# Two of four token tiles project their input from one read of the weights, the second tile's results going through DRAM

## What is computed

```python
proj = rms_norm(h, ln1_g) @ w_in            # [512, 1024] @ [1024, 4096]
u_s5, q, k, v, gate_logits = split(proj)    # 512, 1024, 256, 256, 2048
gates = sigmoid(gate_logits + b_gate)
y_s5 = s5_mixer(u_s5, ...) @ w_s5_branch    # a scan over the tokens
y_attn = sliding_window_attention(q, k, v, ...) @ w_attn_branch
h = h + (g_s5 * y_s5 + g_attn * y_attn) @ w_out
xn2 = rms_norm(h, ln2_g)
# peer_mixer: 8 heads x 16 experts per token, picked by top-k over sub keys
a = einsum('cd,ced->ce', xn2, u_tab[expert])
h = h + einsum('ce,ced->cd', gate * gelu(a), v_tab[expert])
```

## Time and profile before

| what | value |
|---|---|
| runs shown | 3314.36, 3316.03, 3311.30 us; median 3314.36 |
| the profiled execution | 3312.03 us, its span 3310.2 us |
| PE busy, DVE busy | 2458.2 us (74%), 2320.8 us (70%) |
| ACT busy, POOL busy | 1331.3 us (40%), 1137.1 us (34%) |
| DMA | 1295.01 MB, mean 391 GB/s |
| of this, gathers of expert rows | 1076.50 MB, 80.5% of 16 engines' span |
| of this, SP's queue | 213.81 MB, 17.0% |
| chain that ended last | PE 36%, DMA 24%, DVE 22%, issue 10% |

### The profile page before, as it was taken

One profiled execution on the slowest core, in us unless ns is written; L12 is line 12 of the kernel. 1 busy time (PEld: TensorE's weight loads), 2 busy tenths in 40 slices (PEclk: granted clock), 3 DMA queues, 4 the chain that ended last, 5 costly groups with the idle time before them and its releaser, 6 DMA issues.

```text
span 3310.2 us, 40579 instructions
## 1 busy us (share of the span) xinstructions
PE 2458.2 (74%) x14052; PEld 1048.5 (32%) x14052; DVE 2320.8 (70%) x5500; ACT 1331.3 (40%) x3603; POOL 1137.1 (34%) x1038
## 2 busy tenths in 40 slices
PE   7969779786797777879687859778886655555554
PEld 3533333223332233336343426423333211111111
DVE  7429783878738787475975685888866777777644
ACT  2114442444424443243473343368733443333322
POOL 0002342323323243232343343444433444444432
PEclk9979779897898978989888879878888877777877
DMA  8899999999999999999999999999999999999997
GB/s 245 305 354 381 411 384 404 414 409 404 380 403 417 412 396 395 410 375 407 376 370 384 387 395 385 406 416 418 383 405 364 412 420 419 418 413 411 420 420 323
DMA packets 214057, 1295.01 MB, mean 391 GB/s; under 512 B 26934, under 2 KB 30294, under 8 KB 82776
## 3 DMA queue, kind: packets, MB, share of 16 engines
q0 software_dynamic: 148320, 1076.50, 80.5%
q1 hardware_dynamic: 64860, 213.81, 17.0%
q10 hardware_dynamic: 672, 2.12, 0.2%
HBM read 1289.62 MB, written 2.71 MB: 390 GB/s over the span
## 4 chain that ended last, share of the span: by engine, by line
PE 36%; DMA 24%; DVE 22%; issue 10%; ACT 5%; POOL 3%; POOLq 0%; another core or an unknown queue 0%; ACTq 0%; DVEq 0%
PE ps L1714 11%; PE ps L1794 10%; DMA ring<-in_k_uv,idx 10%; DVE ring L413 9%; DMA ring<-in_k_vu,idx 8%; DMA wsl<-in_k_wu 5%; PE ps L2088 5%; POOL ring L2392 3%; PE ps L2098 2%; DVE big L466 2%; ACT L1242 2%; PE ps L1771 1%; PE ps L1969 1%; ACT diag L1242 1%; DMA wsl<-in_k_wmod 1%
## 5 line engine op out<-in xcount | busy, mean ns | idle before, releaser
L1714 PE MATMUL ps<-ring,diag 64*64 64x512 f32 x8192 | 1259.0, 742 | 490.6 <-ACT diag L1242 468.8
L413 DVE CUSTOM_DVE_ANT_0 ring<-ring,xn 128x1024 f32<-128x1024 f32 x1024 | 1237.4, 1220 | 483.7 <-DMA ring<-in_k_vu,idx 259.7
L2392 POOL DMA_INDIRECT ring<-in_k_vu,idx x514 | 566.9, 1103 | 1145.4 <-DVE aw L413 637.1
L2392 POOL DMA_INDIRECT ring<-in_k_uv,idx x510 | 564.1, 1106 | 969.2 <-DVE aw L413 671.7
L1714 PEld LDWEIGHTS ps<-ring,diag 64*64 64x64 f32 x8192 | 313.9, 158 | 1264.3 <-ACT diag L1242 736.6
L1242 ACT ACTIVATE aw<-aw 128x2 f32<-128x2 f32 x512 | 103.6, 202 | 1085.8 <-DVE aw L413 1081.8
L1794 PE MATMUL ps<-wsl,xT 128*128 128x512 f32 x896 | 428.2, 621 | 34.0 <-DMA wsl<-in_k_wu 29.2
L1242 ACT ACT_TABLE_LOAD x340 | 436.2, 1283 | 21.2 <-issue 9.3
L1242 ACT ACTIVATE diag<-gid,aw 128x64 f32<-128x64 f32 x1024 | 311.3, 342 | 298.9 <-PE ps L1714 281.7
L1242 ACT ACTIVATE gid<-ident,gate 128x64 f32<-128x64 f32 x1024 | 292.5, 332 | 0.0
L1794 PEld LDWEIGHTS ps<-wsl,xT 128*128 128x128 f32 x896 | 165.9, 196 | 294.8 <-issue 230.1
(11 more groups left out here) (264 smaller groups left out, 2127.8 us busy)
## 6 DMA issues: line engine op xcount, KB each, us to landing
wsl<-in_k_wu SPq DMA_DIRECT2D x342, 512.0 KB
wsl<-in_k_wmod SPq DMA_DIRECT2D x40, 512.0 KB
ring<-in_k_vu,idx POOLq DMA_INDIRECT x514
ring<-in_k_uv,idx POOLq DMA_INDIRECT x510
ring<-in_k_wmod SPq DMA_DIRECT2D x8, 512.0 KB, 10.0
wsl<-in_k_wu SPq DMA_DIRECT2D x8, 280.0 KB
hres<-in_x SPq DMA_DIRECT2D x4, 512.0 KB, 6.0
pers<-L1d POOLq DMA_DIRECT2D x8, 256.0 KB, 15.7
```

The lines of the kernel that those rows point to most:

```text
L413: V(v.tensor_tensor_reduce(u_row(s), u_row(s), xn[:, n % 3, :], 1.0, 0.0, ALU.mult, ALU.add, aw[:, b, k:k + 1]), ("dot", s))
L1714: r = t.matmul(PA[half][64 * q:64 * q + 64, :], diag[64 * half:64 * half + 64, s % (2 * PAIR), :], v_row(s)[64 * half:64 * half + 64, 512 ...
L2392: Q(p.indirect_dma_start(out=both_rows(s), out_offset=None, in_=tab, in_offset=bass.IndirectOffsetOnAxis(ap=idx[:, n % 2, k:k + 1], axis=0 ...
```

## The change

Tile 3's input projection is done with tile 2's. Its norm follows tile 2's (into a second buffer `xT3`), and the new `project_two` multiplies each unit first with tile 2's, then with tile 3's tokens, banks 4, 5 and 2, 3. ScalarE evicts tile 3's block into one of two buffers (`going`: half of `xr`, and `uT`), waits for its own write and issues a DMA of 256 KB to DRAM (`keptd`). The 32 win units of tile 3 leave the list. SP brings the eight blocks back once tile 2's query has been transposed (so that `xr` is free), ahead of tile 3's first weight, in nine DMAs (block 3 is two). VectorE's copy into `uT` waits for the last two blocks written.

Tiles 2 and 3 get tables of their own: tile 2 from slot 116 to 253, tile 3 from 253 to 360.

```diff
-L1_PARTS = (("norm", 4), ("win", 25), ("qk", 7), ("mid", 48), ("branch", 13), ("route", 10), ("top", 15))
+SHARED_PARTS = (("norm", 5), ("win", 42), ("qk", 7), ("mid", 47), ("branch", 13), ("route", 10), ("top", 13))
+KEPT_PARTS = (("win", 22), ("qk", 6), ("mid", 44), ("branch", 11), ("route", 9), ("top", 15))
...
-        units = [(n,) + u for n in (0, 1, 2, 3, 4, 6) for u in weight_units(n // 4)]
+        units = [(n,) + u for n in (0, 1, 2, 3, 4, 6) for u in weight_units(n // 4) if (n, u[0]) != (3, "win")]
...
-            parts = FIRST_PARTS if n == 1 else L1_PARTS
-            x = (0, -1, 116, 238)[n]
+            parts = (FIRST_PARTS, FIRST_PARTS, SHARED_PARTS, KEPT_PARTS)[n]
+            x = (0, -1, 116, 253)[n]
...
             def u_turned(n):
                 V.stage("qk")
                 V.wait_ge("uT_t", n)
+                if n == 2:
+                    V.wait_ge("kept", 6)
+                    V.wait_ge("kept", 7)
                 V(v.tensor_copy(uT, P3(0)), ("uT", n))
...
+                    if n == 3:
+                        continue
                     S.stage("win")
...
+                    if n == 2:
+                        if b >= 2:
+                            S.wait_ge("kept", b - 2)
+                        S(act(going[b % 2], PS[2 + b % 2], ACT.Copy if b < 4 else ACT.Sigmoid), ("going", b))
+                        S.wait_own()
+                        Q(a.dma_start(keptd[b], going[b % 2]), "kept%d" % (b % 2), ("kept", b))
...
+            def project_two():
+                mine = [u for u in units if u[0:2] == (2, "win")]
+                for k, (_, _, b, u, nk, _, _, nn, _) in enumerate(mine):
+                    pace(2, "win", (k // 2 * 2) / len(mine))
...
+                    for lhsT, bank in ((xT, 4 + b % 2), (xT3, 2 + b % 2)):
+                        if b >= 4 and u == 0:
+                            t.matmul(PS[bank], ones[0:1, :], gt[0:1, 512 * (b - 4):512 * (b - 3)], start=True, stop=False)
+                        for j in range(2):
+                            r = t.matmul(PS[bank], lhsT[:, 2 * u + j, :], wsl[:, at % NWS, j, :],
+                                         start=(u + j == 0 and b < 4), stop=(u * j == 3))
+                    T(r, ("unit_used", at), *([("win", 2, b)] if u == 3 else []))
...
+                if (n, name, b, u) == (3, "glu", 0, 0):
+                    Y.wait_ge("q_t", 2, 1)
+                    for j in range(8):
+                        Y.wait_ge("kept", j)
+                    for j, to in enumerate((xr[:, 0:512], qs[:, 0:512], qs[:, 512:1024])):
+                        Q(s.dma_start(to, keptd[j]), "back0")
```

More of the change, by code:

```diff
@@ L1665, in scalar_program @@
             for n in range(4):
-                norm(n)
+                if n < 3:
+                    norm(n)
+                if n == 2:
+                    norm(3)
                 if n == 0:
@@ L1815, in norm @@
             def norm(n):
-                pace(n, "norm", 0.3)
+                pace(min(n, 2), "norm", 0.3 if n < 3 else 0.8)
                 T.stage("norm")
                 T.wait_ge("xr", n)
-                if n:
+                if n == 3:
+                    T.wait_ge("xT", 2, 1)
+                elif n:
                     T.wait_ge("sS", n - 1, 3)
@@ L2342, in tensor_program @@
                     make_bias(1, 8)
+                if n == 1:
+                    project(n, "win", xk, "win", 0.0, 1.0, ("xT", n, 0), ("xT", n, 1), ("q_e", n - 1, 1))
+                if n == 2:
+                    norm(3)
+                    project_two()
                 if n:
-                    project(n, "win", xk, "win", 0.0, 1.0, ("xT", n, 0), ("xT", n, 1), ("q_e", n - 1, 1))
                     qk1(n)
```

43 lines of the change are left out of this document (35 added, 8 removed).

## The result

| | before | after |
|---|---|---|
| median of four runs each | 3315.2 us (3311.3 to 3318.74) | 3351.92 us (3343.96 to 3355.24) |
| the profiled execution, its span | 3312.03, 3310.2 us | 3355.24, 3353.7 us |
| DMA | 1295.01 MB, mean 391 GB/s | 1282.41 MB, mean 382 GB/s |
| slots 116 to 360 | 803.5 us | 838.3 us |

What follows compares the result with a forecast made beforehand. It took DMA to bind only fronts and tops; with bytes gone, the first front turns TensorE-bound, the second VectorE-bound. Six terms summed to +36.2 us on 3312.0: 3348.2, some 3351 for the median, 8-in-10 range 3316 to 3370.

Steps and rivals of the forecast that it cites:

- 1. tile 2's front and qk: Tile 2's shared front and qk, now 54 slots: TensorE becomes the bound, 207.0 us against 132.9, +74.1 (+67 to +83).
- 2. tile 2's mid: Tile 2's mid, 47 slots for 48: VectorE's chain is the bound, so -1.2 us (to -2.5 at DMA's price).
- 3. tile 2's route and top: Tile 2's route and top: two slots fewer give -5.0 us, blocks read back cost +5.2, together +0.2 (-4 to +4).
- 4. tile 3's front and qk: Tile 3's front and qk, 28 slots for 36: VectorE becomes the bound, DMA idles, 105.6 us, -27.6 (-33 to -23).
- 5. tile 3's mid: Tile 3's mid, 44 slots for 48, at 1.2 us a slot: -4.8 us (to -10 at DMA's price).
- 6. tile 3's branch and route: Tile 3's branch and route, 11 and 9 slots for 13 and 10, at 1.5 us each: -4.5 us (-3 to -7.6).
- The signs that the prediction named: Shared front: TensorE over 95% busy; kept front: VectorE over 90%, GB/s well under 350; slots 116 to 360 near 840 us.
- The sign: At VectorE's copy of uT, end of the shared front: a wait over 15 us would mean that end was sized wrongly.
- A: Faster: DMA stays the bound in both fronts, so the saved bytes show, -36 us, 3278 us; chance 6%.
- B: No change: VectorE's work in tile 3's front hides behind gathers made early, sum about 0, 3314 us; chance 5%.
- C: Less slow: TensorE has room in the shared front, which falls back to DMA's 183 us; +12, 3327 us; chance 8%.
- D: Slower still: the DRAM round trip stalls ScalarE and TensorE in the shared front, some +20 more, 3371 us; chance 5%.

## Why the prediction was right

Forecast 3351.0 us, measured 3351.92; slower, as given the chance of 0.85. Term by term, in us, between the slot borders of the two profiled executions:

| term | predicted | measured |
|---|---|---|
| 1. tile 2's front and qk | +74.1 | 205.1 - 132.9 = +72.2 |
| 2. tile 2's mid | -1.2 | 129.6 - 131.8 = -2.2 |
| 3. tile 2's route and top | +0.2 | 76.4 - 72.8 = +3.6 |
| 4. tile 3's front and qk | -27.6 | 102.6 - 133.2 = -30.6 |
| 5. tile 3's mid | -4.8 | 125.7 - 129.9 = -4.2 |
| 6. tile 3's branch and route | -4.5 | 92.6 - 96.4 = -3.8 |
| sum | +36.2 | +35.0 |

The six terms sum to 35.0 where slots 116 to 360 show 34.8; tile 3's last stage (40.0, as before) and tile 2's branch (66.5, now 66.3) make up the rest. Three of before's stretches in terms 2 and 3, tile 2's mid, route and top, are

```profile
766.40:898.20 131.80, 91.30 (x644) 47.26 (x644) 116.61 (x216) 54.73 (x168) 53.31 (x48) 0.78 0.98 390
964.70:996.90 32.20, 30.55 (x156) 13.02 (x160) 14.26 (x31) 9.94 (x31) 9.30 (x9) 0.90 0.97 382
996.90:1037.50 40.60, 20.03 (x136) 4.95 (x128) 34.36 (x96) 18.63 (x51) 17.24 (x17) 0.81 1.01 420
```

The signs that the prediction named came: TensorE busy 95.6% of the shared front, VectorE 93% of the kept one at 4.0 us a slot and 259 GB/s, no wait for a unit in the first and 2.0 us for a gather in the second. But that the forecast is right to 1 us is luck: terms 3 and 4 missed by 3.4 and 3.0 us in opposite directions, inside term 1 errors of up to 7 us cancel, and the medians differ by 36.7 us where the profiled executions differ by 43.5, of which 8.7 lie outside these slots and show no cause in the change. The pieces of term 1 in the timelines of TensorE, VectorE and ScalarE of after:

```profile
639.61 1.97 PE L1795 MATMUL ps<-ident,xr 128*128 128x128 f32 x8 [2.52 <-DVE xr L474]
648.54 4.43 PE L1738 MATMUL ps<-ring,diag 64*64 64x512 f32 x24 [6.96 <-ACT diag L1253]
652.90 1.09 PE L1795 MATMUL ps<-ident,xr 128*128 128x128 f32 x8
655.04 7.11 PE L1819 MATMUL ps<-wsl,xT 128*128 128x512 f32 x16 [1.04 <-DVE xT L470]
662.07 2.81 PE L1738 MATMUL ps<-ring,diag 64*64 64x512 f32 x24
664.81 7.13 PE L1819 MATMUL ps<-wsl,xT 128*128 128x512 f32 x16
...
816.71 0.66 PE L1795 MATMUL ps<-ident,xr 128*128 128x128 f32 x4
```

```profile
816.06 0.33 ACTq L1393 DMA_DIRECT2D keptd<-big  x1
```

```profile
824.71 0.69 DVE L593 COPY big<-ps 128x512 f32<-128x512 f32 x1 [18.96 <-DMA keptd<-big]
```

- **The start** was taken as 10.5 us and is 15.5, from slot 116 at 639.5 to the first product at 655.0. Tile 3's transposes stand behind slots whose diagonals TensorE waits 6.96 us for: the two norms follow one another, and beside them TensorE has only the products of three slots. Of the 2 to 7.6 us given for it, more than the upper end was spent.
- **TensorE** was taken as 168.5 us without gaps and took 161.7 (655.0 to 816.7). The gapless pattern is there, 7.13 and 2.81 us in turns, as predicted from tile 6. Two units for two tiles take 7.13 us where I had taken twice the 3.70 of one tile, so 16 such groups are 114.1 us and not 118.4; most of the rest is the slots', three in 2.74 us (from 662.07 to 664.81), 0.91 each and not 0.97. The gap of 2.5 us for copying out a tile's sum (at slot 128 here), which the prediction called the ring's evacuation, did not come.
- **The last write** was taken as 5 us beyond the transposes and took 7.3, from 817.4 (816.71 + 0.66) to 824.7; the swap of the buffers gave 5.4 back. The block was issued at 816.06 and had landed 8.6 us later.
- The 19.0 us that VectorE waited at uT is over the 15 that the prediction named as a sign that the end was sized wrongly. Most of it is the wait for TensorE, which the term holds elsewhere: with the swap it is a wait of 12.0 us for the transposes. The sign was badly chosen.

Landing times of the eight blocks:

```profile
DMA to landing us min/median/max: 5.3/8.2/8.6
```

They lie in the range of the output's stores, 2.6 to 9.2 us. By the Trainium skill (DMA: Bandwidth & Descriptors, Anatomy of one DMA) a 256 KB block would land in 2.6 us, an estimate from its fixed time and rate, which it gives for DMAs that GpSimd issues. These were issued by ScalarE, and the trace shows 5.3 to 8.6, beside queues of gathers: the estimate does not hold here.

**Term 3** missed by 3.4 us, nearly the price of the reads. They were taken at 5.2 us and cost 5.7 in the run without the trip; but the two slots that left gave back some 2 us and not 5: without the trip route and top took 31.5 + 39.3 = 70.8, against 72.8 with two slots more. DMA's share in the route stage was 0.91 at 346 GB/s, so gathers did not run ahead there as before; whether that is the cause was not tried.

**Term 4** gave 3 us more than predicted. VectorE came to the copy of uT 83.9 us after slot 253 (1116.9 to 1200.8), not 87: its work was the 81.8 us counted, the waits left were 2.0 us and not 3.9, and the 1 us for the transposes did not come. Then qk took 18.7, as counted (18.6). **Terms 2, 5 and 6** are right within 1 us.

**The rivals.** A (DMA bound in both fronts) fell by the runs with a quarter of the units and without the top-k. B (VectorE's front hides) fell with the kept front's 80.6 busy us. C (TensorE has room) fell by the run without tile 3's products, which was 15.7 us shorter. D (the round trip stalls ScalarE) did not come: ScalarE never waited for a landed block in the front, and the whole trip is 11 us.

**What the prediction had wrong in its reasons.** It said "Only fronts and tops are truly DMA's", and priced the 12.6 MB at 36 us if DMA stayed the bound. For the fronts the first is half the truth: this is the step of the reading that failed, though no term of the sum rested on it. The bytes taken away at no cost gained nothing, and neither did the top-k's 47 us of VectorE: two bounds end together there. What the change undid is the overlap. Before, each win part had 91 us of TensorE, 84 of VectorE and DMA at its full share for all of its 105 to 107 us beside one another; after, one front has 164 us of TensorE beside 106 of VectorE, and the other 81 of VectorE beside 37 of TensorE. The two together went from 105.1 + 107.4 = 212.5 to 171.5 + 87.0 = 258.5 us. Those 46 us hold 14 slots more than before (64 for 50), and the stages that gave them up returned 11, which leaves the 34.8. The Trainium skill (Perfetto Trace Analysis, Optimization Strategy) advises to interleave regimes in which different engines are the most contended. The change took apart two that were interleaved, and the runs agree with the rule: with the slots left as they were, slots 116 to 360 took 44.0 us more, the trip in it (some 11 us in the change's table).

## What to carry to other kernels

- Sharing a read over two tiles also moves the products of both into one stage and empties the other. Sum the longest engine of each stage before and after; bytes count only where DMA is the longest by itself.
- A DMA share of 1.02 didn't prove here that DMA alone was the bound. The chain inside the stretch showed units at 16% and the dots at 19%: when several engines share the chain, expect a second bound right behind the first, and test by taking the bytes away before building a way to save them.
- Price a movable piece of work by stage (here a slot: 1.0 us in the shared front, 1.1 to 1.6 in a mid, 1.8 in the kept front; in a tile's own front 2.6 for slots added to tile 2's, but 1.0, 1.5 and 2.7 for the four taken out of tile 1's, 2's and 3's) and move it to where it is cheapest. Here a change of two tables gained 0.3%, where the saved bytes lost 1.1%.
